# Attention of block 2: bias, floor and reciprocal of both steps of an iteration by one operation each

## The reference

```python
def _masked_softmax(logits, mask):
    l = jnp.where(mask, logits, -jnp.inf)
    m = jnp.max(l, axis=-1, keepdims=True)
    m = jnp.where(jnp.isfinite(m), m, 0.0)
    e = jnp.where(mask, jnp.exp(l - m), 0.0)
    return e / jnp.maximum(jnp.sum(e, axis=-1, keepdims=True), 1e-30)
```

```python
    merge = jax.nn.sigmoid(p['merge'].reshape(B, S, N_BRANCH_2, D_MODEL))
    merged = jnp.sum(merge * jnp.einsum('bsnc,ncd->bsnd', ys, w_branch), axis=2)
    return x + merged @ w_out
```

## Time and profile before

| | before |
|---|---|
| time, median of 3 runs | 3315.37 us (3315.31 to 3318.84) |
| span of the profiled execution | 3315.3 us |
| PE busy | 3209.5 us, 97% |
| DVE busy | 1924.1 us, 58% |
| ACT busy | 1440.5 us, 43% |
| attention, first layer of block 2 | from about 2204 to about 2412 us of the span |
| attention, second layer | from about 2900 to about 3107 us |

### The profile page before, as it was taken

One profiled execution on the slowest core, in us unless ns is written; L12 is line 12 of the kernel. 1 busy time (PEld: TensorE's weight loads), 2 busy tenths in 40 slices (PEclk: granted clock), 3 DMA queues, 4 the chain that ended last, 5 costly groups with the idle time before them and its releaser, 6 DMA issues. The chain is left out here.

```text
span 3315.3 us, 51847 instructions
## 1 busy us (share of the span) xinstructions
PE 3209.5 (97%) x20772; PEld 2547.2 (77%) x20772; DVE 1924.1 (58%) x3355; ACT 1440.5 (43%) x2349; POOL 56.8 (2%) x44
## 2 busy tenths in 40 slices
PE   8999999999999999999999999999999999899998
PEld 6777788788877777788888888767678788566786
DVE  6544745677557447446775373268756652478555
ACT  6423523444246225334443243455643443656632
POOL 0010000000000210000000000000000000000000
PEclk9999999999999999999999999999999999999999
DMA  4324332333333224432333253223153442132342
GB/s 164 90 79 145 140 115 77 108 96 98 111 128 92 79 60 164 163 99 89 95 99 111 70 185 113 86 77 86 38 191 116 133 149 102 63 97 59 142 145 70
DMA packets 107694, 358.37 MB, mean 108 GB/s; under 512 B 12681, under 2 KB 13065, under 8 KB 104785
## 3 DMA queue, kind: packets, MB, share of 16 engines
q1 hardware_dynamic: 107472, 355.33, 33.5%
HBM read 310.57 MB, written 38.81 MB: 105 GB/s over the span
## 5 line engine op out<-in xcount | busy, mean ns | idle before, releaser
L224 PE MATMUL banks<-h_high,weights_high 128*128 128x512 f32 x2448 | 980.9, 401 | 16.9 <-DVE weights_low L245 11.7
L225 PE MATMUL banks<-h_low,weights_high 128*128 128x512 f32 x2448 | 956.9, 391 | 0.0
L226 PE MATMUL banks<-h_high,weights_low 128*128 128x512 f32 x2448 | 956.9, 391 | 0.0
L224 PEld LDWEIGHTS banks<-h_high,weights_high 128*128 128x128 f32 x2448 | 461.1, 188 | 125.7 <-DVE weights_low L245 13.4
L226 PEld LDWEIGHTS banks<-h_high,weights_low 128*128 128x128 f32 x2448 | 460.9, 188 | 98.0
L225 PEld LDWEIGHTS banks<-h_low,weights_high 128*128 128x128 f32 x2448 | 461.6, 189 | 93.0 <-issue 3.3
L1854 DVE TENSOR_TENSOR weights_low<-ring,weights_high 128x1024 fp32r<-128x1024 f32 (+2 forms) x124 | 164.6, 1328 | 292.1 <-ACT weights_high L1800 292.0
L1800 ACT CAST weights_high<-ring 128x1024 fp32r<-128x1024 f32 (+2 forms) x124 | 140.6, 1134 | 437.2 <-PE banks L226 437.0
L217 DVE TENSOR_TENSOR weights_low<-ring,weights_high 128x1024 fp32r<-128x1024 f32 x131 | 161.9, 1236 | 277.9 <-ACT weights_high L212 276.5
L212 ACT CAST weights_high<-ring 128x1024 fp32r<-128x1024 f32 x131 | 137.2, 1048 | 378.7 <-PE banks L226 373.6
L1998 ACT CAST weights_high<-ring 128x1024 fp32r<-128x1024 f32 (+1 forms) x116 | 132.5, 1142 | 322.6 <-PE banks L226 322.6
(11 more groups left out here) (473 smaller groups left out, 4902.0 us busy)
## 6 DMA issues: line engine op xcount, KB each, us to landing
ring<-in_in SPq DMA_DIRECT2D x136, 512.0 KB, 4.2
ring<-in_up SPq DMA_DIRECT2D x88, 512.0 KB, 3.6
ring<-in_gates SPq DMA_DIRECT2D x72, 512.0 KB, 4.2
x<-in_gates SPq DMA_DIRECT2D x56, 512.0 KB, 4.2
ring<-in_down SPq DMA_DIRECT2D x32, 704.0 KB, 4.1
ring<-in_out SPq DMA_DIRECT2D x32, 512.0 KB, 3.6
ring<-in_branch SPq DMA_DIRECT2D x16, 768.0 KB, 4.3
stored<-g_spill SPq DMA_DIRECT2D x16, 768.0 KB, 4.5
```

Of the source, the lines that this page charges most:

```text
L224: pe.matmul(bank, core.wh[:, half, w], high, start=start, stop=False)
L225: pe.matmul(bank, core.wh[:, half, w], low, start=False, stop=False)
L226: return pe.matmul(bank, core.wl[:, half, w], high, start=False, stop=stop)
```

## The change

The bias of A is no longer computed behind A's mask. One operation behind B's mask computes the four biases of A and B (128x2x2 instead of twice 128x2). In the same way one floor and one reciprocal serve the four sums of both steps, and stand behind the exps of both; the gates stay one operation a step. The two L3086 follow at the end, one behind the other. The semaphores `masked` and `inverted` therefore count pairs of steps: `exps` of A, `scale` of A and `logits` wait for the pair.

```diff
--- before.py
+++ after.py
@@ -2957,7 +2957,7 @@
                     return
                 part, i = pair(s), steps[s][1]
                 if s >= 2:
-                    pe.wait_ge(sems["masked"], s - 1)
+                    pe.wait_ge(sems["masked"], s // 2)
                 w = width(s)
                 for h in range(2):
                     mm = pe.matmul(banks[2 * (s % 2) + h][:, 0:w], part["q"][half(h), i * P:(i + 1) * P], part["k"][half(h), 0:w],
@@ -3007,7 +3007,7 @@
             def exps(s):
                 if not has(s):
                     return
-                act.wait_ge(sems["masked"], s + 1)
+                act.wait_ge(sems["masked"], s // 2 + 1)
                 for h in range(2):
                     l = probs[s % 4][:, h, 0:width(s)]
                     act.activation(l, l, ACT.Exp, scale=SCALE, bias=stats[:, s % 4, 2 + h:3 + h],
@@ -3027,7 +3027,7 @@
             def scale(s):
                 if not has(s):
                     return
-                act.wait_ge(sems["inverted"], s + 1)
+                act.wait_ge(sems["inverted"], s // 2 + 1)
                 l = probs[s % 4][:, 1, 0:width(s)]
                 act.mul(l, l, stats[:, s % 4, 5:6]).then_inc(sems["scaled"], 1)
 
@@ -3067,23 +3067,33 @@
                     own(dve.tensor_tensor_reduce(out=probs[s % 4][:, h, 0:w], in0=banks[2 * (s % 2) + h][:, 0:w],
                                                  in1=pair(s)["mask"](h, steps[s][1]), scale=1.0, scalar=NEG * 1e-5, op0=ALU.add,
                                                  op1=ALU.max, accum_out=stats[:, s % 4, h:h + 1]))
+
+            def both_steps(s, at):
+                return stats[:, s % 4:s % 4 + 2, at:at + 2]
+
+            def biases(s):
+                if not has(s):
+                    return
                 own.settle()
-                dve.tensor_scalar(stats[:, s % 4, 2:4], stats[:, s % 4, 0:2], -SCALE, None, ALU.mult).then_inc(sems["masked"], 1)
+                dve.tensor_scalar(both_steps(s, 2), both_steps(s, 0), -SCALE, None, ALU.mult).then_inc(sems["masked"], 1)
 
             def normalise(s):
                 if not has(s):
                     return
-                dve.wait_ge(sems["exped"], 2 * s + 2)
-                sums = stats[:, s % 4, 4:6]
+                dve.wait_ge(sems["exped"], 2 * s + 4)
+                sums = both_steps(s, 4)
                 own(dve.tensor_scalar(sums, sums, 1e-30, None, ALU.max))
                 own.settle()
                 own(dve.reciprocal(sums, sums))
                 own.settle()
-                if pair(s)["row"] is not None:
-                    own(dve.tensor_tensor(sums, sums, pair(s)["row"](steps[s][1]), ALU.mult))
+                for n in (s, s + 1):
+                    if pair(n)["row"] is not None:
+                        one = stats[:, n % 4, 4:6]
+                        own(dve.tensor_tensor(one, one, pair(n)["row"](steps[n][1]), ALU.mult))
                 own.tell(sems["inverted"])
-                l = probs[s % 4][:, 0, 0:width(s)]
-                dve.tensor_scalar(l, l, stats[:, s % 4, 4:5], None, ALU.mult).then_inc(sems["ready"], 1)
+                for n in (s, s + 1):
+                    l = probs[n % 4][:, 0, 0:width(n)]
+                    dve.tensor_scalar(l, l, stats[:, n % 4, 4:5], None, ALU.mult).then_inc(sems["ready"], 1)
 
             def output(s):
                 if has(s) and s in finished:
@@ -3114,10 +3124,10 @@
                 output(2 * d - 1)
                 mask(2 * d + 2)
                 mask(2 * d + 3)
+                biases(2 * d + 2)
                 if d == -1:
                     extra_low(dve, sems, core, e, 1)
                 normalise(2 * d + 2)
-                normalise(2 * d + 3)
                 extra_lows(dve, sems, core, e, ("last", d - 1))
                 if 0 <= d < rounds:
                     rank(d)
```

## The result

The changed kernel takes 3346.55 us (median of 4 runs, 3344.36 to 3348.14) against 3317.11 us before in the same comparison (3315.31 to 3320.98): 1.0087 of before, with a 95% interval from 1.0074 to 1.0100. It is slower by 29 us; 3343 us was forecast. The span of its profiled execution is 3342.5 us, 27.2 us more than before. That execution took 3344.36 us, 1.9 us more than its span, so a time and a span may not be set side by side to 0.1 us, as was done for the kernel before; differences of times and differences of spans may.

What follows compares the result with a forecast made beforehand. PE bounds the first stretch of each attention, a DVE-ACT loop the second; 5.7 + 8.0 = 13.7 us a layer, 27.4 for both, added to 3315.3 gives 3342.7, so 3343 us, between 3335 and 3349 (64%).

Steps and rivals of the forecast that it cites:

- The path of one iteration: Iteration 14: exps A, copies and exps B each start 1.0 us later, L3086 of A adds 0.3; next mask A 1.3 us late.
- Iterations 11 to 16: Stretch where the DVE-ACT loop binds: 8.0 us lost a layer, taken over fully by PE once its waits for copies begin.
- my rule: One turn of the DVE-ACT loop: lateness grows by the time from bias A to bias B, less 0.17, plus 0.27 us.
- the gaps: Times from bias A to bias B before the change; 7.7 us summed over iterations 11 to 16, 9.3 over 1 to 10.
- Iterations 0 to 10: Stretch where ACT has some air: 5.7 us of DVE lateness a layer when iteration 11 begins, entering the sum whole.
- the late starts: Exps A starting later than usual after bias A in four of iterations 1 to 10, absorbing 1.7 us of lateness.
- near 8 to 11: Sign: the iterations in which PE's waits for the copies L3025 should begin in the first layer.
- Iterations 17 to 23: Last stretch: PE busy throughout, lateness stays; scale of A some 0.5 us behind exps B, transposes later than that; nothing added.
- the 18 I named: Sign: PE's wait for the copies L3025 in the first layer should go from 5.6 us to about 18.
- saved DVE time shortens the loop: Rival: 12 turns of iterations 11 to 16, both layers, each save three small operations, 0.5 us: 3309 us; 3%.
- only the second stretch pays: Rival: DVE's lateness from iterations 0 to 10 is drained there, 16 us remain in both layers: 3331 us; 15%.
- The clock's part: Rival: PE's clock falls behind four or five longer waits a layer, about 1 us each uncovered: 3352 us; 13%.

## Why the prediction was right, step by step

**The path of one iteration** held in its sum, 1.26 us against the 1.3 forecast (DVE's lateness at the start of the search round, iteration 14 less iteration 13), but not in its parts. From the row of bias B to that of the common bias iteration 14 is 7.41 us later (2349.70, 2357.11), from exps A to exps A 8.61, from floor B to the common floor 8.60. So the shift that passes through exps and copies is 1.20 us, the whole gap: the bias that was taken out ahead of mask B saved nothing here, where I had taken off 0.17. And the L3086 of A added only 0.1 us, from 8.60 at the floor to 8.69 at the search round (2353.43, 2362.12), where I had put 0.27: before, DVE's next operation L1335 started at 2352.29, right behind the end of ACT's L1310 (2352.26), and I take it that this wait had hidden the rest.

**Iterations 11 to 16** were forecast at 8.0 us and cost 8.7. DVE's lateness at the start of the search round, counted from the head start, was 3.7 us in iteration 10, then 5.7, 7.0, 9.1, 10.4 and 11.7 in the iterations 11 to 15: 8.0 us in five turns, where my rule sums to 7.3. The two turns of 512 and 384 columns gave 2.06 and 2.12 us against 1.82 by the rule, and iteration 15 gave 1.32 against 1.04. Both terms of the rule were a little too small. At the floor of B the six iterations add 1.70, 1.17, 1.71, 1.17, 0.69 and 0.69 us, 7.1 in all, where the gaps less six biases are 6.7: in fox the removed bias saved next to nothing, in mem 0.25 us. Behind the floor the five turns add 0.35, 0.09, 0.41, 0.09 and 0.63 us, 1.6 in all, where 5 x 0.27 is 1.35: step A is 512 columns wide in iterations 11 and 13, and I had priced every L3086 by one of 256. In iteration 15 L3096 starts 0.53 us behind the reciprocal and not 0.18, which I cannot explain. At PE the last `values` of the stretch is 10.70 us later (2367.94, 2378.64), 12.4 us with the head start; the forecast had 13.7.

**Iterations 0 to 10** are the term that was mis-sized: 3.7 us of lateness instead of 5.7. It grew as the rule says in iterations 3, 4, 9 and 10, where ACT has no idle time, but fell back in 5 and 6 (2.1, 2.0, 1.7 us), where the sum has it stand. Carried turn by turn through iterations 1 to 10, three terms were each somewhat off. Exps of A fell behind by 5.2 us, where the gaps less the biases and the late starts give 5.9. Ahead of exps B 4.9 us of that were absorbed, where I took off 4.2: in each of the six iterations in which ACT had stood idle, about 0.1 more than that idle time. L3096 and the gates added 3.2 us, where I had 3.7. PE kept its pace up to iteration 8, and its first wait for the copies came in iteration 9, inside the "near 8 to 11" that was named. Changed alone, this stretch costs 0.30%, so it belongs in the sum.

**Iterations 17 to 23** were put at nothing, and that step failed: PE lost another 2.8 us in each layer, in the first from 12.4 to 15.2. Of these, 0.9 us come at once, behind the last wait for the copies (2.48 us). The eight `logits` there, before and after, and the granted clock in a window over each:

```profile
2368.53 1.13 PE L2963 MATMUL banks<-mem_k,queries 64*128 64x256 f32 x8
2368.00:2370.00 2.00, 1.66 (x16) 1.04 (x16) 1.14 (x5) 2.00 (x6) 0.00 (x0) 1.00 0.00 0
...
2379.23 1.93 PE L2963 MATMUL banks<-mem_k,queries 64*128 64x256 f32 x8
2380.00:2382.00 2.00, 2.00 (x11) 1.27 (x9) 1.82 (x4) 1.46 (x4) 0.00 (x0) 0.50 0.00 0
```

The clock was at its lower level, and the logits took 0.8 us more; the transposes and the products behind them were slower as well. Before, the transposes then waited 0.66 us for L3086, which takes up a part, and no wait for the copies follows that could take up the rest. Most of the remaining loss, 1.3 us, comes ahead of iteration 23. The timelines of DVE and PE after show it:

```profile
2419.86 0.17 DVE L3085 TENSOR_SCALAR stats<-stats 128x4 f32<-128x4 f32 x1 [3.32 <-ACT probs L3013]
2420.42 0.82 DVE L3096 TENSOR_SCALAR probs<-probs,stats 128x384 f32<-128x384 f32 x2 [0.18 <-DVE stats L3087]
...
2421.07 0.84 PE L2976 MATMUL banks<-con_sb,probs 128*128 128x128 f32 x6 [1.04 <-DVE probs L3096]
```

The floor of A started at 2403.86 us before and is the common floor at 2419.86 now, 16.0 us later, while that of B is 13.2 us later (2406.67 before). The first transposes of the next iteration need A alone, and wait 1.04 us. I had seen this delay for `scale` and called the transposes late enough; with few product blocks beside them they are not. That the kernel with the common form up to iteration 15 gives nothing back there bears this out.

In the first layer the three stretches were 2.0 us too much, 0.7 too little and 2.8 too little, so the sum, 13.7 forecast and 15.2 measured, is nearer than its parts, and that is luck. For both layers 27.4 us stand against 29.4 between the medians and 30.0 in the pairs; the remaining 1.7 us between 3343 and 3346.55 are the median before, which is 3317.1 in this comparison and was 3315.4. The 13.0 us of PE's waits for the copies are less than the 18 I named, and the longest is 2.6 us, not 3: part of the loss appears elsewhere, 2.5 us in the matmuls of the transposes that wait for L3096 and 5.5 us in matmuls that took longer.

**The rivals.** That saved DVE time shortens the loop is out, since DVE's busy time fell and its waits rose by more. That only the second stretch pays is out by the change in the iterations up to 10 alone. The clock's part is seen but not settled: the windows of the changed kernel have a granted clock of 0.97 up to 2335 us and 0.87 from there to 2381, where the earlier trace rows has 0.99 and 0.91 for about the same iterations, and over the whole kernel the same matmuls are busy 7.4 us longer (3209.5, 3216.9). Where the loop binds, PE's next wait can take such time up, and I count only the 0.9 us above as surely lost through the clock; no run here held the waits and changed the clock alone.

```profile
core 0: us, PE busy (x) PEld busy (x) DVE busy (x) ACT busy (x) POOL busy (x), PEclk, DMA share, GB/s
2204.00:2335.00 131.00, 123.37 (x740) 90.47 (x738) 88.69 (x327) 69.38 (x205) 0.00 (x0) 0.97 0.30 85
2335.00:2381.00 46.00, 34.36 (x212) 24.00 (x208) 30.38 (x109) 24.12 (x73) 0.00 (x0) 0.87 0.10 29
```

Of the rules in the Trainium skill that were weighed, that of the page "Perfetto Trace Analysis", section "Optimizing Scalar/DVE Operations", on breaking instructions up where an unsaturated engine makes bubbles on others, agrees for the bias: 0.56% lies between two kernels that differ only in the place of a bias of 0.17 us. For floor and reciprocal it does so only beside the common bias (0.3%): making them common by itself cost 0.07%, within the interval of no change. The Trainium skill's rule of fewer operations, "VectorE: DVE Perf Modes", section "Rules for kernel authors", gave nothing measurable by itself, 1.0055 merged against 1.0056 unmerged.

## What to carry to other kernels

Before merging small operations of two steps, ask what the first step's result releases on another engine: the price of the merge is not the operation but all the work that now stands between that result's inputs and its signal. Where two engines hand a step back and forth, look for work of the waiting engine that needs neither and lay it into the wait; here moving one search round gained 0.3%, and merging could then be had at no loss that the runs can tell. A stretch with cover still passes its lateness on to the first stretch without, so carry lateness turn by turn and do not stop where the engine in question has air.

## What the runs showed of the hardware

DVE operations on 128x4 and 128x2 of f32 in SBUF take nearly the same time: 171 against 169 ns for a TENSOR_SCALAR, 179 against 166 ns for a RECIPROCAL. The latter before:

```profile
L3080 DVE RECIPROCAL stats<-stats 128x2 f32<-128x2 f32 x48 | 8.0, 166 | 1.6
```

Two biases of two columns side by side cannot be told from one of four in the kernel's time, 3335.56 and 3334.06 us, inside each other's spread of runs.

Eight matmuls of 64x256 took 1.93 us behind a wait of 2.48 us of PE, at a granted clock of 0.50 (1.2 GHz), and 1.13 us at 1.00.
